# Softmax sums divided out once per pair of heads, on GpSimd by way of DRAM; four loads and one store moved to ScalarE's queue

## The chip, the cores and the metric

One core of a Trainium2 chip runs the program in one launch. The metric is device time in microseconds (us). The kernel before takes 1885.9 us (median of 3 runs, 1885.32 to 1886.08).

## The reference

One layer of a streaming encoder on x (1 x 1024 x 1024, fp32) and a conditioning vector c:

```
mod = silu(c) @ w_ada + b_ada                    # 9 vectors of 1024: shift, scale, gate, three times
h = rms(x) * (1 + scale) + shift;  x += 0.5 * gate * swiglu(h)        # FFN 1, D_FF = 2816
h = rms(x) * (1 + scale) + shift;  x += gate * mixer(h)
h = rms(x) * (1 + scale) + shift;  x += 0.5 * gate * swiglu(h)        # FFN 2
out = rms(x) * g_final

mixer:  p = h @ w_in                             # q, k, v of 8 attention heads x 64; q, k, v, o of 4 mLSTM heads x 128; gates
        first attention ("fox"):  logits = q k^T / 8 + cum(i) - cum(j), causal;  y_a = softmax(logits) v
        mLSTM ("ml"):  chunks of the matrix memory, causal conv before, norm and sigmoid gate after -> y_b
        return [y_a, y_b] @ w_out
```

## The kernel before

**Order.** Five engine programs run the parts one after another: FFN 1 (with the modulation of the start), mixer, output projection, FFN 2. Each fp32 product is three fp32r products, high x high, high x low and low x high; ScalarE cuts the high parts (`w_cut_hi`, `cut_hi`), VectorE or GpSimd the low ones (`w_cut_lo`, `cut_lo`). All order is written out by hand in the engines' programs and held by semaphores. There is no planner. All DMAs are issued by SyncE (SP), in one queue.

**First attention.** `mixer` goes through 4 pairs of heads (`PAIRS`), each with 8 blocks of 128 queries (`NS`), the longest block (1024 keys) first. For a block q of a pair p:
- TensorE: `scores` (L2872) of both heads into PSUM. `turn_prob` (L2887) transposes the exponentials by 128x128 pieces. `values` (L2903) multiplies the transposed pieces with v and gives y, by feature, in bank 6 + q % 2, columns 0 to 127. `turn_rinv` (L2909) transposes the inverse sums into columns 128 to 255 of the same bank. Projections of the next pair's q and k (L2132 to L2134) are put between.
- VectorE: `logits` (L2595) adds the decay rows `cum_bc` and takes the minimum; `invert` (L2614) makes the inverse of the row sums, spread over 128 columns; `keep_pt` (L2607) moves part of the transposed pieces; `normalise` (L2621) multiplies y by the turned inverses and writes `yT_fox`.
- ScalarE: `exp_rows` (L2385) with the row sums, `keep_pt` (L2393), `keep_rinv` (L2399), `keep_qk` (L2376 for k, L2374 for q).
- GpSimd: `mask_block` (L2287), one per block, on the causal block of `cum_bc`; it waits for the logits of the block before. At blocks 1 and 2 also one `w_cut_lo` (L2124). After the last pair: two `w_cut_lo` of the mLSTM's v weights, three of head weights, then the other mask `mask_m` (L2318, L2320), which VectorE awaits at L2690.
- SP: `fox_loads` per pair: wait for all logits of the pair before, load `cum_bc`, load the next pair's q and k weights; in pair 0 then spill x to `x_spill`. After the four pairs, four loads of v weights, then `head_load`, which waits for the low cuts of the pieces before it.

A block's y frees its bank by `y_done`. `values` of block q waits for `y_done` of block q - 2, and after the pair `project_q0` for all eight.

**Start.** `Start.load` issues the small rows, then x tiles 0 to 3 (L640) alternating with four pieces of w_ada (L636), then four more pieces, FFN 1's first weights (L432), and the second half of pieces. ScalarE squares and scales the x tiles (`act_lead`). VectorE sums the pieces (`dve_sum`, L808 to L816). FFN 1's first product (L1042 to L1044) needs both.

**End.** Output tiles 4 to 7 go out as halves: the right one scaled by ScalarE (`scale_half`, L1510), the left one by VectorE (L1733). SP issues all eight (L1378).

Of the kernel before, what the change touches and what calls it, by code (L numbers as in the profile page):

```python
# [14 lines left out]
P = 128  # L15
# [551 lines left out]
class Start:  # L567
# [55 lines left out]
    def load(self, sp, first_weights):  # L623
        KD, D = self.c.KD, self.c.D
        sp.dma_start(self.brow[2 * KD:, :], self.c_vec.rearrange("a (k p) -> (a k) p", p=P))\
            .then_inc(self.small_loaded, 16)
        sp.dma_start(self.brow[0:2 * KD, :], self.b_ada[:, 0:2 * D].rearrange("a (r n) -> (a r) n", n=P))\
            .then_inc(self.small_loaded, 16)
        columns = self.w_ada[0, :, 0:2 * D].rearrange("a (v h n) -> h a v n", v=2, h=2)

        def piece(half, k):
            if half:
                self.wait_piece(sp, 0, k)
                if k >= 4:
# [4 lines left out]
        def tile(t):  # L639
            sp.dma_start(self.c.xres[:, t, :], self.x[0, t * P:(t + 1) * P, :]).then_inc(self.x_loaded[t], 16)  # L640

        for k in range(4):
            tile(k)
            piece(0, k)
        for k in range(4, KD):
            piece(0, k)
        first_weights(0)
        for k in range(KD):
            piece(1, k)
        first_weights(1)  # L650
        for t in range(4, self.c.NS):
            tile(t)
# [87 lines left out]
    def act_lead(self, act):  # L740

        c, KD = self.c, self.c.KD
        act.wait_ge(self.b_turned, 1)
# [500 lines left out]
def ffn(core, tag, buf, halved, weights, w_out, spill, x_dram, gate_row, next_mod=None, g_final=None, out=None,  # L1244
# [53 lines left out]
    def sync(sp):  # L1298
# [71 lines left out]
        else:  # L1370
# [8 lines left out]
            sp.wait_ge(stored, 16 * (NS + 4))  # L1379
# [43 lines left out]
    def scalar(act):  # L1423
# [88 lines left out]
        if next_mod is None:  # L1512
# [13 lines left out]
            for t in (6, 7):  # L1526
                scale_half(t)
        else:
# [442 lines left out]
def mixer(core, ms, w_mix_in, b_fox_f, b_m_i, b_m_f, w_conv, b_conv, g_mhn, w_mix_out,  # L1971
# [57 lines left out]
    rinv_made, rinv_kept = s("rinv_made"), s("rinv_kept")  # L2029
# [48 lines left out]
    rinv = core.at("mx_rinv", [P, 4, P], 120)  # L2078
# [129 lines left out]
    def sync(sp):  # L2208
# [6 lines left out]

        def fox_loads(p, first, last):
# [11 lines left out]
        repeat(sp, PAIRS, fox_loads)  # L2228
        for piece in range(4):
            w_load(sp, piece % 2, C_MV[0] + piece // 2, w_in[:, 2 * piece:2 * piece + 2, COL_MV:COL_MV + MW])  # L2230

# [35 lines left out]
    def gpsimd(pool):  # L2267
# [49 lines left out]
        pool.wait_ge(y_done, PAIRS * NS)  # L2317
# [32 lines left out]
    def scalar(act):  # L2350
# [44 lines left out]
        def keep_rinv(p, q, first):  # L2395
            act.wait_ge(pv_ready, p * NS + (q + 1))
            if not (first and q < 2):
                act.wait_ge(y_done, p * NS + (q - 1))
            act.copy(rinv[:, 2 + q % 2, :], core.bank[:, 6 + q % 2, P:2 * P]).then_inc(rinv_kept, 1)  # L2399

        def fox_body(p, first, last):
            for q in range(1, NS + 1):
# [16 lines left out]
                if q > 1:  # L2419
                    keep_rinv(p, q - 2, first)  # L2420
                if q < NS:
                    keep_pt(p, 2 * q - 1, first)
            keep_rinv(p, NS - 1, first)
# [35 lines left out]
        def ml_body(h, first, last):  # L2459
# [27 lines left out]
            if h == 1:  # L2487
                act.wait_ge(x_spilled, NS * 16)
                for k in range(PAIRS):
# [39 lines left out]
    def vector(dve):  # L2529
# [79 lines left out]
        def invert(p, q, first):  # L2609

            dve.wait_ge(prob_done, p * PER + (2 * q + 2))
            if not (first and q < 2):
                dve.wait_ge(pv_ready, p * NS + (q - 1))
            dve.reciprocal(rinv[:, q % 2, :].rearrange("p (e d) -> p e d", e=2),  # L2614
                           rowsum[:, 2 * q:2 * q + 2].unsqueeze(2).to_broadcast([P, 2, HD]))\
                .then_inc(rinv_made, 1)

        def normalise(p, q):
            dve.wait_ge(rinv_kept, p * NS + (q + 1))
            i = BLOCK[2 * q]  # L2620
            dve.tensor_tensor(yT_fox[:, bass.ds(p, 1), i * P:(i + 1) * P].rearrange("p a s -> p (a s)"),  # L2621
                              core.bank[:, 6 + q % 2, 0:P], rinv[:, 2 + q % 2, :], ALU.mult).then_inc(y_done, 1)

        def fox_body(p, first, last):
            link.at(p)
            for q in range(1, NS + 1):
# [13 lines left out]
                if q > 1:  # L2640
                    normalise(p, q - 2)
            normalise(p, NS - 1)
# [149 lines left out]
    def tensor(pe):  # L2792
# [98 lines left out]
        def values(p, q, first):  # L2891
# [9 lines left out]
            for j in range(i + 1):  # L2901
                for e in range(2):
                    pe.matmul(bank[e * HD:(e + 1) * HD, 0:P], v_fox[:, j, bass.ds(p * (2 * HD) + e * HD, HD)],  # L2903
                              pt_of(2 * q + e, j * P, (j + 1) * P), start=(j == 0), stop=(j == i))
# [12 lines left out]
        def fox_body(p, first, last):  # L2917
            project_q0(p, first, range(2 if first else 0, KD - 2))
            for q in range(1, NS):
                scores(p, q, first)  # L2920
                if q in (6, 7):
                    values(p, q - 2, first)
                    turn_rinv(p, q - 2)
                    turn_prob(p, 2 * q - 2, first)
                else:
# [3 lines left out]
                    else:  # L2929
                        values(p, q - 2, first)  # L2930
                        turn_rinv(p, q - 2)
# [17 lines left out]
            turn_rinv(p, NS - 2)  # L2949
            turn_rinv(p, NS - 1)  # L2950
# [497 lines left out]
```

## Time and profile before

| | us |
|---|---|
| median of 3 runs | 1885.9 |
| the profiled execution's own time | 1886.72 |
| its span (first to last instruction) | 1885.0 |
| TensorE busy | 1856.6 (98%) |
| VectorE busy | 1183.5 (63%) |
| ScalarE busy | 764.7 (41%) |
| GpSimd busy | 841.3 (45%) |
| mean granted TensorE clock | 0.995 |

In the rows below, PE is TensorE, PEld its weight load, DVE VectorE, ACT ScalarE, POOL GpSimd, SPq the DMA issues of SyncE. Times are us from the start of the span, and L12 is line 12 of the kernel. Square brackets hold an engine's idle time before an instruction, and what ended it. "issue" there means that it waited for nothing that the profile shows. Matmuls are pipelined, so that the distance between two starts tells more than their durations. Busy shares of TensorE near 100% say that it has work queued, not that it runs at its peak.

The first attention lies at about 755 to 945 us; a pair takes about 50 us.

### The profile page before, as it was taken

The page shows a single profiled execution, that of the slowest core. Times are in us where ns is not written, and L with a number is a line of the kernel's source. Part 1 is how long each engine was busy: PE and PEld are TensorE (multiplying, and loading weights), DVE is VectorE, ACT ScalarE, POOL GpSimd, SP SyncE. Part 2 cuts the span into 40 slices and gives each one's busy share as a digit, 9 for nine tenths or more (in the row PEclk, how much of TensorE's full clock was granted, in tenths as well). Part 3 has the DMA queues.
Part 4 walks back from the last instruction along what each step waited for, and adds up shares of the span by engine and source line. Part 5 has one row for each costly group of instructions (what it writes and reads, how often), then busy time and mean ns, then how long its engine had stood idle before and what let it go on. Part 6 is the DMA issues. An engine that isn't in the chain of part 4 may idle for free.

```text
span 1885.0 us, 25322 instructions
## 1 busy us (share of the span) xinstructions
PE 1856.6 (98%) x9100; PEld 1527.7 (81%) x9100; DVE 1183.5 (63%) x1763; ACT 764.7 (41%) x1439; POOL 841.3 (45%) x635
## 2 busy tenths in 40 slices
PE   7999999999999999999999999999999999999998
PEld 6888888888888878777788888878888888888886
DVE  6966777666777782555604567477634454368678
ACT  5643232332444552555513555352333323334445
POOL 1588877783000111222222332699877887700003
PEclk8999999999999999999999999999999999999999
DMA  9346666654976401301112123424322422178652
GB/s 341 101 139 206 188 205 201 181 179 144 389 237 190 124 24 42 136 27 46 68 49 70 45 68 127 175 95 128 107 95 90 130 100 101 46 292 312 209 192 90
DMA packets 213379, 267.95 MB, mean 142 GB/s; under 512 B 16100, under 2 KB 126856, under 8 KB 212744
## 3 DMA queue, kind: packets, MB, share of 16 engines
q1 hardware_dynamic: 213256, 266.34, 42.4%
q8 instruction: 73, 1.20, 0.2%
q14 instruction: 50, 0.41, 0.1%
HBM read 211.17 MB, written 53.03 MB: 140 GB/s over the span
## 4 chain that ended last, share of the span: by engine, by line
PE 87%; DVE 5%; POOL 4%; issue 2%; ACT 1%; SPq 1%; DMA 1%; DVEq 0%; ACTq 0%; POOLq 0%
PE bank L1768 13%; PE bank L1769 13%; PE bank L1770 13%; PE bank L1202 6%; PE bank L1200 6%; PE bank L1201 6%; PE bank L2132 5%; PE bank L2134 5%; PE bank L2133 5%; PE bank L2903 2%; PE bank L2887 2%; PE bank L2872 1%; PE bank L1042 1%; PE bank L1043 1%; PE bank L1044 1%
## 5 line engine op out<-in xcount | busy, mean ns | idle before, releaser
L510 POOL TENSOR_TENSOR ffn_ring_b<-ffn_raw_in,ffn_ring_b 128x512 fp32r<-128x512 f32 x146 | 204.8, 1411 | 98.9 <-ACT ffn_ring_b L505 98.8
L1200 PE MATMUL bank<-ffn_w_hi,ffn_a_hi 128*128 128x512 f32 x616 | 239.7, 389 | 0.0
L1201 PE MATMUL bank<-ffn_w_lo,ffn_a_hi 128*128 128x512 f32 x616 | 239.6, 389 | 0.0
L1202 PE MATMUL bank<-ffn_w_hi,ffn_a_lo 128*128 128x512 f32 x616 | 239.6, 389 | 0.0
L132 POOL TENSOR_SCALAR rms<-rms 128x1 f32<-128x1 f32 x20 | 9.0, 449 | 427.5 <-ACT ffn_junk L124 419.6
L1155 ACT CAST ffn_a_hi<-ffn_a_stage 128x512 fp32r<-128x512 f32 x154 | 95.6, 621 | 200.7 <-PE bank L1202 195.4
L505 ACT CAST ffn_ring_b<-ffn_raw_in 128x512 fp32r<-128x512 f32 x150 | 92.4, 621 | 199.1 <-PE bank L1770 192.6
L510 POOL TENSOR_TENSOR ffn_ring_a_lo<-ffn_raw_in,ffn_ring_a_hi 128x512 fp32r<-128x512 f32 x106 | 146.5, 1393 | 54.9 <-ACT ffn_ring_a_hi L505 52.8
L1166 DVE TENSOR_TENSOR ffn_a_lo<-ffn_a_stage,ffn_a_hi 128x512 fp32r<-128x512 f32 x154 | 106.3, 690 | 72.1 <-ACT ffn_a_hi L1155 71.9
L2124 POOL TENSOR_TENSOR mx_w_lo<-mx_raw_w,mx_w_hi 128x1024 fp32r<-128x1024 f32 x25 | 59.8, 2390 | 176.8 <-ACT mx_w_hi L1886 113.3
L1547 DVE TENSOR_TENSOR ffn_u<-bank,ffn_u 128x512 f32<-128x512 f32 x103 | 70.8, 688 | 107.5 <-PE bank L1770 106.8
L1200 PEld LDWEIGHTS bank<-ffn_w_hi,ffn_a_hi 128*128 128x128 f32 x616 | 115.7, 188 | 24.4 <-DVE ffn_w_lo L1166 0.4
L1202 PEld LDWEIGHTS bank<-ffn_w_hi,ffn_a_lo 128*128 128x128 f32 x616 | 115.7, 188 | 24.0
L1201 PEld LDWEIGHTS bank<-ffn_w_lo,ffn_a_hi 128*128 128x128 f32 x616 | 115.7, 188 | 23.9
L1768 PE MATMUL bank<-h_hi,ffn_ring_a_hi 128*128 128x512 f32 x340 | 133.0, 391 | 1.1 <-DVE ffn_g L1547 0.5
L1770 PE MATMUL bank<-h_hi,ffn_ring_a_lo 128*128 128x512 f32 x340 | 132.3, 389 | 0.0
L1769 PE MATMUL bank<-h_lo,ffn_ring_a_hi 128*128 128x512 f32 x340 | 132.3, 389 | 0.0
L1769 PE MATMUL bank<-f_t_lo,ffn_ring_b 128*128 128x512 f32 x340 | 132.3, 389 | 0.0
L1768 PE MATMUL bank<-h_hi,ffn_ring_b 128*128 128x512 f32 x332 | 130.0, 392 | 0.4 <-ACT ffn_g L1431 0.2
L1770 PE MATMUL bank<-h_hi,ffn_ring_b 128*128 128x512 f32 x332 | 129.3, 389 | 0.0
L2132 PE MATMUL bank<-h_hi,mx_w_hi 128*128 128x512 f32 x296 | 118.5, 400 | 0.0
L1768 PE MATMUL bank<-f_t_hi,ffn_ring_b 128*128 128x512 f32 x300 | 116.8, 389 | 0.6 <-DVE f_t_lo L340 0.6
(427 smaller groups left out, 4690.1 us busy)
## 6 DMA issues: line engine op xcount, KB each, us to landing
ffn_raw_in<-in_w_ffn_in SPq DMA_DIRECT2D x84, 512.0 KB, 5.9
ffn_a_stage<-hidden SPq DMA_DIRECT2D x154, 256.0 KB, 3.6
ffn_w_stage<-in_w_ffn_out SPq DMA_DIRECT2D x132, 256.0 KB, 3.5
ada_rest<-in_w_ada SPq DMA_DIRECT2D x64, 448.0 KB, 3.8
hidden<-ffn_u SPq DMA_DIRECT2D x87, 256.0 KB, 2.0
hidden<-ffn_g SPq DMA_DIRECT2D x66, 256.0 KB, 2.0
mx_raw_w<-in_w_mix_in SPq DMA_DIRECT2D x28, 512.0 KB, 4.6
xres<-in_x SPq DMA_DIRECT2D x16, 512.0 KB, 8.1
```

What stands on the lines that cost most here:

```text
L510: pool.tensor_tensor(self.lo(q), self.source(b, m), self.hi(q).bitcast(F32), ALU.subtract)\
L1155: act.copy(self.op(self.buf.a_hi, n), self.a_source(n)).then_inc(self.hi_done, 1)
L1166: dve.tensor_tensor(self.op(lo, n), source, self.op(hi, n).bitcast(F32), ALU.subtract)\
L1200: pe.matmul(dst, a_hi, w_hi, start=first, stop=False, skip_group_check=True)
L1201: pe.matmul(dst, a_hi, w_lo, start=False, stop=False, skip_group_check=True)
L1202: return pe.matmul(dst, a_lo, w_hi, start=False, stop=True, skip_group_check=True)
L1768: pe.matmul(dst, w_hi, h_hi, start=(fresh and k == 0), stop=False, skip_group_check=True)
L1769: pe.matmul(dst, w_hi, h_lo, start=False, stop=False, skip_group_check=True)
L1770: mm = pe.matmul(dst, w_lo, h_hi, start=False, stop=(k == 3), skip_group_check=True)
L2132: pe.matmul(dst, a_hi, b_hi, start=start, stop=False, skip_group_check=skip)
L2133: pe.matmul(dst, a_hi, b_lo, start=False, stop=False, skip_group_check=skip)
L2134: return pe.matmul(dst, a_lo, b_hi, start=False, stop=stop, skip_group_check=skip)
```

## The change

Three things:
1. **Attention.** `invert` writes two numbers per token and block instead of 128. `turn_rinv`, `keep_rinv` and `normalise` go; VectorE copies the undivided y out of PSUM (`keep_y_fox`), and the last matmul of `values` carries `pv_ready`. After each pair SP stores the pair's 2048 inverses to DRAM, by token (one element of 4 bytes each), waits for the store, and loads them back as rows spread over 64 partitions per head (`spread_inverse`). GpSimd multiplies the pair's yT_fox by them, in place, in one instruction of 128x1024 (`divide`): behind block 4's mask of the next pair, and for the last pair behind the three head cuts, ahead of `mask_m`. SP's loop over the pairs is written out.
2. **Start.** x tiles 0 to 3 are issued by ScalarE, ahead of its first activation; SP issues the pieces of w_ada back to back.
3. **End.** The right halves of output tiles 6 and 7 go out as one DMA issued by ScalarE.

```diff
@@ Start.load / act_lead
-        for k in range(4):
-            tile(k)
-            piece(0, k)
-        for k in range(4, KD):
+        for k in range(KD):
             piece(0, k)
@@
+        for t in range(4):
+            self.load_tile(act, t)
         act.wait_ge(self.b_turned, 1)
@@ end of FFN 2: SP, then ScalarE
                 for half, done, n in ((1, half_scaled, t - 3), (0, norm.scaled, t + 1)):
+                    if half and t > 5:
+                        continue
@@
+            act.wait_ge(half_scaled, 4)
+            act.dma_start(out[0, 6 * P:8 * P, BANK:D].rearrange("(t p) d -> p t d", p=P), core.xres[:, 6:8, BANK:D])\
+                .then_inc(stored, 16)
@@ mixer
-    rinv = core.at("mx_rinv", [P, 4, P], 120)
+    rinv = core.at("mx_rinv", [P, PAIRS, 2 * NS], 120)
+    rinv_bc = core.at("mx_rinv_bc", [P, S], 16)
+    rinv_rows = nc.dram_tensor("rinv_rows", (PAIRS * 2 * S,), F32, kind="Internal").ap()
@@ SP
+        def spread_inverse(pairs):
+            before = pairs - 1
+            sp.wait_ge(rinv_made, pairs * NS)
+                sp.dma_start(rinv_rows[bass.ds(before * (2 * S), 2 * S)].rearrange("(n t) -> t n", t=P),
+                             rinv[:, bass.ds(before, 1), :].rearrange("p a n -> p (a n)")).then_inc(rinv_stored, 16)
+            sp.wait_ge(rinv_stored, pairs * 16)
+            sp.wait_ge(x_spilled, NS * 16)
+            if pairs > 1:
+                sp.wait_ge(y_divided, pairs - 1)
+            for e in range(2):
+                sp.dma_start(rinv_bc[e * HD:(e + 1) * HD, :],
+                             rinv_rows[bass.ds(before * (2 * S) + e * S, S)].partition_broadcast(HD)).then_inc(rinv_loaded, 16)
@@ fox_loads, behind the next pair's weights; and once behind the four loads of v weights
+            if not first:
+                spread_inverse(p)
@@ GpSimd
+        def divide(pairs):
+            part = yT_fox[:, bass.ds(pairs + -1, 1), :].rearrange("p a s -> p (a s)")
+            pool.wait_ge(y_done, pairs * NS)
+            pool.wait_ge(rinv_loaded, pairs * 32)
+            pool.tensor_tensor(part, part, rinv_bc[:, :], ALU.mult).then_inc(y_divided, 1)
@@ fox_cut
                 mask_block(p, q)
+                if q == 4 and not first:
+                    divide(p)
@@ after the head cuts
-        pool.wait_ge(y_done, PAIRS * NS)
+        divide(PAIRS)
         pool.memset(mask_m[:, :], 0.0).then_inc(late_mask_set, 1)
@@ ScalarE: keep_rinv and its calls are gone; it awaits y_divided before it reads yT_fox in head 1
@@ VectorE
-            if not (first and q < 2):
-                dve.wait_ge(pv_ready, p * NS + (q - 1))
-            dve.reciprocal(rinv[:, q % 2, :].rearrange("p (e d) -> p e d", e=2),
-                           rowsum[:, 2 * q:2 * q + 2].unsqueeze(2).to_broadcast([P, 2, HD]))\
-                .then_inc(rinv_made, 1)
+            inverse = rinv[:, bass.ds(p, 1), :].rearrange("p a (e i) -> p (a e) i", e=2)[:, :, i:i + 1]
+            dve.reciprocal(inverse, rowsum[:, 2 * q:2 * q + 2].unsqueeze(2)).then_inc(rinv_made, 1)
-        def normalise(p, q):
-            dve.wait_ge(rinv_kept, p * NS + (q + 1))
-            dve.tensor_tensor(yT_fox[...], core.bank[:, 6 + q % 2, 0:P], rinv[:, 2 + q % 2, :], ALU.mult).then_inc(y_done, 1)
+        def keep_y_fox(p, q):
+            dve.wait_ge(pv_ready, p * NS + (q + 1))
+            dve.tensor_copy(yT_fox[...], core.bank[:, 6 + q % 2, 0:P]).then_inc(y_done, 1)
@@ TensorE
+            mm.then_inc(pv_ready, 1)
-        def turn_rinv(p, q):
-            bank = core.bank[:, 6 + q % 2, :]
-            pe.wait_ge(rinv_made, p * NS + (q + 1))
-            pe.transpose(bank[:, P:2 * P], rinv[:, q % 2, :], core.ident[:, :]).then_inc(pv_ready, 1)
```

## Rows read from the trace of the kernel before

**Rows 1.** The page's chain that ended last, shares of the span by engine.

```profile
PE 87%; DVE 5%; POOL 4%; issue 2%; ACT 1%; SPq 1%; DMA 1%; DVEq 0%; ACTq 0%; POOLq 0%
```

**Rows 2.** Busy time by stretch: length, engines (x instructions), clock, DMA share, GB/s.

```profile
28.00:30.00 2.00, 2.00 (x6) 1.56 (x5) 2.00 (x4) 1.94 (x4) 0.00 (x0) 0.50 1.05 407
...
800.00:850.00 50.00, 49.66 (x391) 39.30 (x390) 26.76 (x76) 25.76 (x62) 10.58 (x10) 1.00 0.12 39
...
1883.00:1884.00 1.00, 0.00 (x0) 0.00 (x0) 0.00 (x0) 0.00 (x0) 0.00 (x0) 0.50 1.03 399
```

**Rows 3.** TensorE's waits, 755 to 1160: us in total, times, longest.

```profile
PE bank L3007 <- POOL mx_w_lo L2124: 0.9, 3, 0.3
PE bank L2872 <- DVE mx_fk_lo L2572: 0.7, 3, 0.2
```

**Rows 4.** Timeline, block 2 of pair 0: start, duration, engine, line.

```profile
766.69 1.97 PE L2903 MATMUL bank<-mx_probT,mx_v_fox 128*64 128x128 f32 x32
...
768.59 0.33 PE L2909 MATMUL bank<-ident,mx_rinv 128*128 128x128 f32 x1
...
768.75 0.93 PE L2887 MATMUL bank<-ident,mx_prob 128*128 128x128 f32 x7
...
769.61 0.50 PE L2872 MATMUL bank<-mx_fk_hi,mx_fq_hi 64*128 64x512 f32 x2
```

**Rows 5.** Timeline, end of pair 1.

```profile
854.46 0.50 PE L2872 MATMUL bank<-mx_fk_hi,mx_fq_hi 64*128 64x512 f32 x2 [0.23 <-DVE mx_fk_lo L2572]
```

**Rows 6.** Timeline, end of the last pair.

```profile
943.77 0.44 PE L2909 MATMUL bank<-ident,mx_rinv 128*128 128x128 f32 x2
...
943.97 0.48 PE L2132 MATMUL bank<-mx_w_hi,h_hi 128*128 128x512 f32 x1
```

**Rows 7.** Groups of instructions by line, 755 to 945.

```profile
L2614 DVE RECIPROCAL mx_rinv<-mx_rowsum 128x128 f32<-128x128 f32 x32 | 30.4, 949 | 0.7 <-ACT mx_prob L2385 0.7
```

**Rows 8.** Timeline, GpSimd and VectorE in pairs 0 and 1.

```profile
765.96 0.95 DVE L2595 CUSTOM_DVE_ANT_0 mx_prob<-bank,mx_cum_bc 128x768 f32<-128x768 f32 x1
...
767.32 0.95 DVE L2595 CUSTOM_DVE_ANT_0 mx_prob<-bank,mx_cum_bc 128x768 f32<-128x768 f32 x1
...
767.75 2.37 POOL L2124 TENSOR_TENSOR mx_w_lo<-mx_raw_w,mx_w_hi 128x1024 fp32r<-128x1024 f32 x1 [2.90 <-ACT mx_w_hi L1886]
...
827.33 0.73 POOL L2287 TENSOR_TENSOR mx_cum_bc<-mx_cum_bc,mx_mask_m 128x256 f32<-128x256 f32 x1 [3.15 <-DVE mx_low L2595]
```

**Rows 9.** Timeline, SP in pair 2, GpSimd and ScalarE after the pairs.

```profile
848.39 1.00 SPq L1875 DMA_DIRECT2D mx_raw_w<-in_w_mix_in  x2
...
953.64 2.39 POOL L2124 TENSOR_TENSOR mx_w_lo<-mx_raw_w,mx_w_hi 128x1024 fp32r<-128x1024 f32 x1 [17.31 <-ACT mx_w_hi L1886]
...
971.55 1.05 ACT L1886 CAST mx_w_hi<-mx_raw_w 128x1024 fp32r<-128x1024 f32 x1 [9.83 <-PE bank L2134]
```

**Rows 10.** DMA issues: operands, queue, count, KB each, us to landing.

```profile
gate_rows<-mx_rows_out SPq DMA_DIRECT2D x1, 48.0 KB, 1.5
...
ffn_shift_columns<-mod_rows SPq DMA_DIRECT2D x1, 4.0 KB, 6.7
```

**Rows 11.** Timeline, first mLSTM head.

```profile
997.98 0.17 DVE L2690 TENSOR_TENSOR mx_tiny<-mx_m_max,mx_mst 128x8 f32<-128x8 f32 x1 [5.93 <-POOL mx_mask_m L2320]
...
1001.47 2.60 DVE L2707 SCALAR_TENSOR_TENSOR mx_mkT<-mx_pre_k,mx_consts,mx_mkT 128x1024 f32<-128x1024 f32 x2
...
1006.10 4.62 DVE L2707 SCALAR_TENSOR_TENSOR mx_mqT<-mx_pre_q,mx_consts,mx_mqT 128x1024 f32<-128x1024 f32 x2
...
1020.24 1.15 ACT L2481 ACTIVATE mx_mkT<-mx_mkT,mx_consts 128x1024 f32<-128x1024 f32 x1
```

**Rows 12.** Timeline, the start.

```profile
0.80 1.28 ACT L744 ACT_TABLE_LOAD   x1 [0.80 <-PEq L3437]
...
1.65 0.41 SPq L640 DMA_DIRECT2D xres<-in_x  x1
...
15.40 1.28 DVE L816 SCALAR_TENSOR_TENSOR ada_lead_acc<-ada_ring,c_act,ada_lead_acc 128x1024 f32<-128x1024 f32 x1 [0.61 <-DMA ada_ring<-in_w_ada]
```

More of the change, by code:

```diff
@@ L651, in load, with load_tile @@
         for t in range(4, self.c.NS):
-            tile(t)
+            self.load_tile(sp, t)
+    def load_tile(self, eng, t):
+        eng.dma_start(self.c.xres[:, t, :], self.x[0, t * P:(t + 1) * P, :]).then_inc(self.x_loaded[t], 16)
     def sums_by(self, pieces):
@@ L1378, in sync @@
                     sp.dma_start(out[0, t * P:(t + 1) * P, cols], core.xres[:, t, cols]).then_inc(stored, 16)
-            sp.wait_ge(stored, 16 * (NS + 4))
+            sp.wait_ge(stored, 16 * (NS + 3))
     def gpsimd(pool):
@@ L2214, in sync @@
         sp.wait_ge(rows_stored, 16)
+        def spread_inverse(pairs):
+            before = pairs - 1
+            sp.wait_ge(rinv_made, pairs * NS)
+            with nc.allow_non_contiguous_dma(reason="inverse sums by token, 16 columns"):
+                sp.dma_start(rinv_rows[bass.ds(before * (2 * S), 2 * S)].rearrange("(n t) -> t n", t=P),
[7 more added lines that the diff above has]
+                             rinv_rows[bass.ds(before * (2 * S) + e * S, S)].partition_broadcast(HD)).then_inc(rinv_loaded, 16)
         def fox_loads(p, first, last):
@@ L2226, in fox_loads @@
                     sp.dma_start(x_spill[t * P:(t + 1) * P, :], core.xres[:, t, :]).then_inc(x_spilled, 16)
-        repeat(sp, PAIRS, fox_loads)
+        for p in range(PAIRS):
+            fox_loads(p, p == 0, p == PAIRS - 1)
         for piece in range(4):
             w_load(sp, piece % 2, C_MV[0] + piece // 2, w_in[:, 2 * piece:2 * piece + 2, COL_MV:COL_MV + MW])
+        spread_inverse(PAIRS)
         def head_load(m):
@@ L2393, in keep_pt @@
             act.copy(pt_of(n, 0, w), turned_bank(n, 0)[:, 0:w]).then_inc(pt_act, 1)
-        def keep_rinv(p, q, first):
-            act.wait_ge(pv_ready, p * NS + (q + 1))
-            if not (first and q < 2):
-                act.wait_ge(y_done, p * NS + (q - 1))
-            act.copy(rinv[:, 2 + q % 2, :], core.bank[:, 6 + q % 2, P:2 * P]).then_inc(rinv_kept, 1)
         def fox_body(p, first, last):
@@ L2611, in invert @@
             dve.wait_ge(prob_done, p * PER + (2 * q + 2))
-            if not (first and q < 2):
-                dve.wait_ge(pv_ready, p * NS + (q - 1))
-            dve.reciprocal(rinv[:, q % 2, :].rearrange("p (e d) -> p e d", e=2),
-                           rowsum[:, 2 * q:2 * q + 2].unsqueeze(2).to_broadcast([P, 2, HD]))\
-                .then_inc(rinv_made, 1)
-        def normalise(p, q):
-            dve.wait_ge(rinv_kept, p * NS + (q + 1))
-            i = BLOCK[2 * q]
-            dve.tensor_tensor(yT_fox[:, bass.ds(p, 1), i * P:(i + 1) * P].rearrange("p a s -> p (a s)"),
-                              core.bank[:, 6 + q % 2, 0:P], rinv[:, 2 + q % 2, :], ALU.mult).then_inc(y_done, 1)
+            i = BLOCK[2 * q]
+            inverse = rinv[:, bass.ds(p, 1), :].rearrange("p a (e i) -> p (a e) i", e=2)[:, :, i:i + 1]
+            dve.reciprocal(inverse, rowsum[:, 2 * q:2 * q + 2].unsqueeze(2)).then_inc(rinv_made, 1)
+        def keep_y_fox(p, q):
+            dve.wait_ge(pv_ready, p * NS + (q + 1))
+            i = BLOCK[2 * q]
+            dve.tensor_copy(yT_fox[:, bass.ds(p, 1), i * P:(i + 1) * P].rearrange("p a s -> p (a s)"),
+                            core.bank[:, 6 + q % 2, 0:P]).then_inc(y_done, 1)
         def fox_body(p, first, last):
@@ L2640, in fox_body @@
                 if q > 1:
-                    normalise(p, q - 2)
-            normalise(p, NS - 1)
+                    keep_y_fox(p, q - 2)
+            keep_y_fox(p, NS - 1)
             if not last:
@@ L2902, in values @@
                 for e in range(2):
-                    pe.matmul(bank[e * HD:(e + 1) * HD, 0:P], v_fox[:, j, bass.ds(p * (2 * HD) + e * HD, HD)],
-                              pt_of(2 * q + e, j * P, (j + 1) * P), start=(j == 0), stop=(j == i))
-        def turn_rinv(p, q):
-            bank = core.bank[:, 6 + q % 2, :]
-            pe.wait_ge(rinv_made, p * NS + (q + 1))
-            pe.transpose(bank[:, P:2 * P], rinv[:, q % 2, :], core.ident[:, :]).then_inc(pv_ready, 1)
+                    mm = pe.matmul(bank[e * HD:(e + 1) * HD, 0:P], v_fox[:, j, bass.ds(p * (2 * HD) + e * HD, HD)],
+                                   pt_of(2 * q + e, j * P, (j + 1) * P), start=(j == 0), stop=(j == i))
+            mm.then_inc(pv_ready, 1)
         def first_mv(t, ks):
```

13 lines of the change are left out of this document (3 added, 10 removed).

## The prediction

> **What bounds the kernel now.** I read the chain of waits first: 87% of the span is TensorE's own work [rows 1]. So a change saves time only where it shortens TensorE's queue, or where TensorE waits. Then the table by stretch, for the attention: in 50 us TensorE is busy 49.66 at clock 1.00, while VectorE has 26.8 and ScalarE 25.8 [rows 2]. Then TensorE's waits from 755 to 1160: the two longest groups come to 0.9 and 0.7 us [rows 3]. The attention is bound by TensorE's instruction stream, not by the engines that the change relieves. Last I read the timeline around each instruction that goes or is moved, and the first and last 30 us, where DMA is the bound: 407 GB/s at 28 to 30 us, 399 in the last full microsecond of the end [rows 2].
>
> **The change part by part.**
>
> *TensorE, the 32 transposes of inverse sums.* What one costs is its slot, not its 0.33 us. In a block the 32 matmuls of values begin 0.055 apart ((1.97 - 0.27 of the last) / 31), so the last begins at 768.39; the transpose begins at 768.59 and the next real one at 768.75 [rows 4]. So the last matmul of values and turn_prob are 0.36 apart. Without turn_rinv a wait still stands between them, that of turn_prob. What such a boundary costs is seen one step on: the seven transposes (0.11 apart) have their last start at about 769.41, and scores begin at 769.61, 0.20 later; values to turn_rinv is 0.20 too [rows 4]. So the boundary stays at 0.20 and each transpose gives back 0.16. Blocks 2 to 7 of each of the 4 pairs have one such place (turn_rinv of the block two before): 24 x 0.16 = 3.8 us. The other two transposes of a pair come at its end. In pairs 0 to 2 TensorE waits there for VectorE's low cut of k (scores at 854.46, idle 0.23 for fk_lo) [rows 5], which follows from the projection and not from the transposes: 3 x 0. In the last pair nothing is awaited: 943.77 to 943.97, 0.20 us [rows 6]. Sum 4.0 us. Bounds: nothing, if the next wait (ScalarE's copy of the piece before) ends no earlier; or the whole 0.36 at 24 places and 0.4 at the last, 9 us, if the boundary closes too. I take 4.0, since both boundaries in the row agree, and in block 2 the copy that turn_prob awaits had ended 0.4 us ahead of it.
>
> *VectorE and ScalarE.* invert shrinks from 949 ns [rows 7] to about 0.17 (an operation of 8 columns takes 0.17 [rows 11]), 32 x 0.78 = 25 us of VectorE; 32 copies of ScalarE go (0.26 each in the timeline); normalise becomes a copy of the same size. All of it lies beside TensorE's stream, so I put it at 0. It widens margins: y_done comes earlier, and nobody waited for it. A gain of up to 0.7 us is possible where TensorE awaited fk_lo [rows 3]; a loss I exclude, for both engines only get less.
>
> *SP, spread_inverse.* In pairs 1 to 3 it stands behind the next weights, which are issued by 849.4 in pair 2 [rows 9]; SP's next task is a pair (50 us) away, so its waits hold up nobody there. What matters is when the rows land. No row shows a store of 2048 single elements. From both sides: 48 KB of rows stored took 1.5 us; 1024 single elements loaded took 6.7, behind 1 MB of other loads [rows 10]. So 1.5 to 13.4 (twice 6.7); I take 4, nearer to the store. With the load back (5 us at most for 512 KB; the larger loads of this shape took 4.9 in the DMA table) the rows are there 9 us after 849.4, 18 us at the latest, 868. divide comes at 874.5 in that pair. Hidden. After the last pair SP waits at about 941 for the last inverses, and head_load(0) behind it waited until 956 in any case, for the cut that began at 953.64 [rows 9]. So 15 us of store cost nothing; even then the weight is first cut at 971.55, 10 us after it lands [rows 9]. Cost 0.
>
> The Trainium skill says in "DMA: Bandwidth & Descriptors" (Rules for kernel authors; Specifications) that a strided last dimension becomes one descriptor per element and that transfers under 512 B are read, changed and written back. It speaks against this store, and no row here shows such a store. By it the store would lie at the slow end; the sum stays until some 20 us, and this rule is why the slow store below has a chance at all.
>
> *GpSimd, divide.* A tensor_tensor of 128x1024 takes 2.37 [rows 8]. In pair 1 it stands between mask 4 (ends about 824.2) and mask 5, which begins at 827.33 after 3.15 us of idling [rows 8]: it fits with 0.7 us to spare, in pairs 1 to 3 alike. Without that cover it would put up to 2.4 us in front of VectorE's logits, three times. The last one goes ahead of mask_m: VectorE, idle 5.93 us for the mask, goes on at 1000.4 instead of 997.98; its convolution of k ends near 1007.7, and ScalarE takes it up at 1020.24 [rows 11]. 12 us of cover. Cost 0.
>
> GpSimd may also slow VectorE: a pair of convolution steps takes 2.60 alone and 4.62 beside a GpSimd cut [rows 11]. But logits of the same width take 0.95 without and 0.95 beside a GpSimd operation of 2.37 [rows 8]. divide runs beside logits. Cost 0, upper end 2.0 a pair.
>
> By the skill's "GPSIMD Engine Reference" (Key points) the two engines contend where VectorE has two SBUF inputs. Logits have one, the other being PSUM, and the convolution has two; the trace agrees with both (0.95 and 0.95; 2.60 and 4.62). By this rule the three divides are free, and the last one might lengthen a convolution that has 12 us.
>
> *Start.* ScalarE could begin its work at 0.80 [rows 12], SP issued the first tile at 1.65 [rows 12], and from about 3 us on DMA is the bound. The stream can begin up to 0.85 earlier; the order of bytes (tile and piece by turns) stays. VectorE's sums awaited a piece at 15.40 [rows 12] and ran densely from there to FFN 1's first product at 27.3, so an earlier piece counts. But TensorE runs at 0.50 until about 32 [rows 2], and if that moment doesn't move, only about half of the lead is kept (a matmul of 512 columns comes every 0.43 there and every 0.23 after it). The four issues push the table load back by 2 us, c_act from 3.3 to some 4.1; its first use was at 6.9, when the piece had landed. I take 0.5; bounds -0.85 of gain and 0.5 of loss (if tiles and pieces get in each other's way).
>
> *End.* All data were ready at 1880.6, and the last issue at 1881.7; that looks like 1 us to gain. But the 16 engines ran at 383 to 414 GB/s from 1880 until 1884 (399 in the last of the four [rows 2]). The same bytes remain, so 0 (bounds -0.3 and +0.3).
>
> **Sum.** 4.0 + 0 + 0.5 + 0 = 4.5 us off the profiled execution's span of 1885.0 and its own time of 1886.72, so 1882.2 for it. It lay 0.8 above the median; 1885.9 - 4.5 = 1881.4.
>
> **The rivals.**
> 1. *The boundary closes too* (the 0.20 also goes, or VectorE's relief shortens waits called "issue"): 9 + 0.5, 1876.4. For it: the gap isn't named by any releaser. Against: it is 0.20 behind values and behind transposes alike [rows 4].
> 2. *The next wait takes its place*: turn_prob needs ScalarE's copy; TensorE's stream then is no shorter, and only the start remains: 1885.4. Against: the 0.4 us margin in block 2, and more in the later blocks.
> 3. *GpSimd's divide stalls VectorE* (other side): in block 4 to 5 of pairs 1 to 3, logits stretched as the convolution is, 3 x 2.0, and mask 5 pushed by what exceeds 0.7 us of room, 3 x 1.0 more when GpSimd itself gets slower by that much. 1885.9 - 4.5 + 6.0 = 1887.4, to 1890.4. It decides from 1.5 us a pair (4.5 / 3). Against: 0.95 and 0.95 [rows 8].
> 4. *The store is slow*: free up to 20 us in the pairs and about 24 after the last; from there every us counts fully, 30 us would give 1881.4 + 6 + 3 x 10 = 1917. Each of 16 engines has 128 elements, so it would need 0.16 us an element; 6.7 us for 1024 of them [rows 10] says less than 0.11 even with all of the queue ahead charged to them.
> 5. *The start's half clock moves*: the 12 matmuls at half clock cost 12 x 0.20 = 2.4 us; with them gone 1879.0, with as many more 1883.8. The clock there fell while TensorE had few matmuls, and the new order of arrivals changes these.
>
> **Chances.** Forecast 0.60 (own range 1880 to 1883), rival 1 0.10, rival 2 0.12, rival 3 0.06, rival 4 0.02, rival 5 0.10. A range from 1877.5 to 1884.5 takes in the forecast, rival 5 and part of 1 and 2. What a measurement can tell from no change is 0.2%, 3.8 us: faster means below 1882.1. The forecast is near that line: three quarters of its 0.60, rival 1 and half of rival 5 give 0.60 faster; slower takes rival 4 and most of rival 3, 0.07; the same is the rest, 0.33.
>
> **What would show it.** L2909 gone, and the last matmul of values and turn_prob 0.20 apart (0.36: rival 2; 0.06: rival 1). A pair at 49.3 instead of 50.3 us. Mask 5 without a later start relative to the logits before it, and logits of 512 columns at 0.69 beside divide (longer: rival 3). The store's landing between 1.5 and 13.4 us. The first FFN matmul at 26.5 to 27.3. The last byte out at the same distance from the last matmul as before. The prediction is wrong if TensorE's waits in the attention pass 2 us, or if the pair's length doesn't change.

## The result, and the profile after

The changed kernel takes 1890.3 us (median of 9 runs, 1889.69 to 1892.37); the kernel before took 1885.81 beside it (9 runs, 1884.9 to 1886.85). The ratio is 1.0025, 95% interval 1.0016 to 1.0033: slower by 4.5 us, where 1881.4 and a gain of 4.5 were forecast. The measurement also lies outside the range of 1877.5 to 1884.5.

Its profiled execution took 1889.85, with a span of 1887.6. I set the two traces side by side at three places: the first scores of the attention, the first scores of the last pair, and TensorE's first matmul behind the last values and transposes (943.97 before [rows 6], 946.36 after).

| stretch of the span, us | before | after | difference |
|---|---|---|---|
| to the first scores | 755.04 | 753.03 | -2.01 |
| pairs 0 to 2 (scores to scores) | 149.77 | 147.84 | -1.93 |
| last pair, to the first matmul behind it | 39.16 | 45.49 | +6.33 |
| from there to the end | 941.03 | 941.24 | +0.21 |

The first two parts gained, the start more than its forecast of 0.5, the three pairs less than theirs (18 x 0.16 = 2.9). The part behind the pairs hardly moved. The last pair lost three times what either of the first two gained. The place is seen in TensorE's waits from 740 to 1030 (us in total, times, longest), which answer to [rows 3]:

```profile
PE bank L2912 <- issue: 5.5, 1, 5.5
PE bank L2897 <- DVE mx_fk_lo L2599: 1.8, 3, 0.6
```

One new wait of 5.5 us, put down to "issue": TensorE waited for a semaphore whose release the profile does not name. The timeline of that moment shows what it was. In the kernel before, SP issued the v weights early in this pair, and ScalarE cut them without waiting:

```profile
898.39 66.19 SPq L1875 DMA_DIRECT2D mx_raw_w<-in_w_mix_in  x6
...
910.24 1.03 ACT L1886 CAST mx_w_hi<-mx_raw_w 128x1024 fp32r<-128x1024 f32 x1
```

SP's queue in the last pair of the changed kernel (start, duration, line, operands):

```profile
895.37 0.37 SPq L2228 DMA_DIRECT2D rinv_rows<-mx_rinv  x1
907.23 1.09 SPq L2235 DMA_DIRECT2D mx_rinv_bc<-rinv_rows  x2
908.37 15.74 SPq L1879 DMA_DIRECT2D mx_raw_w<-in_w_mix_in  x4
```

and TensorE and ScalarE around that wait, then TensorE behind the pair:

```profile
908.21 1.09 PE L2912 MATMUL bank<-ident,mx_prob 128*128 128x128 f32 x8
...
906.20 0.18 ACT L2420 ACTIVATION_READ_ACCUMULATOR mx_prob<-mx_prob,mx_low 128x1 f32 x1
914.58 1.04 ACT L1890 CAST mx_w_hi<-mx_raw_w 128x1024 fp32r<-128x1024 f32 x1 [8.20 <-DMA mx_raw_w<-in_w_mix_in]
915.53 0.58 ACT L2428 COPY mx_probT<-bank 128x512 f32<-128x512 f32 x1
...
916.21 1.94 PE L2912 MATMUL bank<-ident,mx_prob 128*128 128x128 f32 x8 [5.51 <-issue]
...
946.36 0.50 PE L2139 MATMUL bank<-mx_w_hi,h_hi 128*128 128x512 f32 x1
```

Read from the top: SP stores the inverse sums of pair 2 and waits for them, 895.37 to 907.23. Behind it in SP's program stand, in this pair, the four loads of the v weights, which the kernel before issued from 898.39 on and this one at 908.37. ScalarE's program has the cut of these weights between an exponential and the copy keep_pt. It comes to the cut at 906.4 and waits 8.20 us for the DMA. TensorE's next transposes need the bank that keep_pt empties: the copy begins at 915.53, and they begin at 916.21. TensorE has stopped for 5.51 us of ScalarE's 8.20, so it had 2.7 us of cover. Behind the stall the granted clock is down (columns: the stretch, its length, TensorE busy and its instructions, clock, DMA share, GB/s):

```profile
905.00:910.00 5.00, 5.00 (x33) 1.00 0.27 81
910.00:915.00 5.00, 0.70 (x4) 0.79 0.74 234
915.00:920.00 5.00, 3.79 (x20) 0.52 0.01 2
920.00:925.00 5.00, 5.00 (x62) 1.00 0.16 25
```

At 915 to 920 it is 0.52, next to the lower of the two levels, 1.2 of 2.4 GHz: the transposes at 916.21 take 1.94 us for eight, 1.09 for eight at full clock at 908.21.

The DMA table of the page (operands, queue, count, KB each, us to landing) shows what held SP, and the count of packets shows why:

```profile
DMA packets 222257, 270.06 MB, mean 143 GB/s; under 512 B 24468, under 2 KB 135224, under 8 KB 221624
rinv_rows<-mx_rinv SPq DMA_DIRECT2D x4, 8.0 KB, 13.3
mx_rinv_bc<-rinv_rows SPq DMA_DIRECT2D x8, 256.0 KB, 3.9
```

Before, 16100 packets were under 512 B. The 8368 more are the 4 x 2048 elements of the stores and 176 others. By "DMA: Bandwidth & Descriptors" (Rules for kernel authors) of the Trainium skill a strided last dimension becomes one descriptor per element; the traces agree. Run 2 below, which differs from the changed kernel only in storing rows of 16 adjacent elements (512 rows instead of 8192 elements), has 7679 packets under 512 B fewer than the changed kernel, and run 7, which stores 2048 single elements once, has 2065 more than the kernel before.

### The profile page after: what moved, and what is told of

Same layout as the page of the kernel before. It is cut to its first block, busy times and chain, and to the rows that moved or that the text cites. A ratio compares the mean times of both kernels' runs of the same rounds, so it can differ in the third digit from the quotient of the medians.

```text
span 1887.6 us, 25171 instructions
## 1 busy us (share of the span) xinstructions
PE 1853.4 (98%) x9068; PEld 1525.1 (81%) x9068; DVE 1157.8 (61%) x1763; ACT 758.0 (40%) x1407; POOL 849.4 (45%) x639
## 4 chain that ended last, share of the span: by engine, by line
PE 87%; DVE 4%; POOL 4%; issue 2%; DMA 1%; ACT 1%; SPq 0%; DVEq 0%; ACTq 0%; POOLq 0%
PE bank L1772 13%; PE bank L1773 13%; PE bank L1774 13%; PE bank L1199 6%; PE bank L1200 6%; PE bank L1201 6%; PE bank L2139 5%; PE bank L2141 5%; PE bank L2140 5%; PE bank L2912 2%; PE bank L2897 2%; PE bank L2928 2%; POOL out_xn L157 1%; PE bank L3317 1%; PE bank L3315 1%
```

## The experiments

Each was timed against the kernel before on the same chip (its medians there: 1884.92 for the first four, 1884.78 for the next four, 1885.1 for the last). My theory after the traces: the wait on the store, ahead of the v weights, is the whole loss. The rivals: something in the change itself (the divide, GpSimd's order) slows the last pair; or the clock does, for a reason of its own.

**1. The call moved behind the first two v weights.**

```
-            if not first:
+            if not first and not last:
                 spread_inverse(p)
...
         for piece in range(4):
             w_load(...)
+            if piece == 1:
+                spread_inverse(PAIRS - 1)
```

> The changed kernel, with one call moved: the third spread_inverse stands behind the issues of the first two pieces of the v weights instead of ahead of all four. Theory (the store of the inverse sums, 10.5 to 15.4 us to its landing, holds SP and with it the v weights, ScalarE's cut of them waits 8.20 us in its in-order stream and TensorE's pieces of turned probabilities with it): TensorE's stall at 911 to 920 and the half clock behind it go, the last pair falls from 44.75 to about 37.5 us and the time by 7.2, from 1890.3 to 1883.1 (1882 to 1884.5). Rival A (the last pair is slow because of the divide or of GpSimd's order, not of SP's): the pair stays over 42 us, time over 1888. Rival B (the clock falls there for another reason): the stall goes but some 2 us of half clock stay, 1885.

Measured: 1881.26 (1880.52 to 1881.67), 3.66 below the kernel before, ratio 0.998 [0.9971, 0.9989]. Against the changed kernel, each taken from its own kernel before, that is 4.5 + 3.66 = 8.1 us. The expected 1883.1 was missed by 1.8, and the time lies below the expected range: about 0.9 of it is that the kernel before ran 0.9 faster here (1884.92 against 1885.81), and 0.9 that the stall costs 8.1 by the medians, where the expectation reckoned with 7.2. SP's queue, then ScalarE and TensorE in the same pair:

```profile
892.91 0.95 SPq L1879 DMA_DIRECT2D mx_raw_w<-in_w_mix_in  x2
893.90 0.56 SPq L2228 DMA_DIRECT2D rinv_rows<-mx_rinv  x1
907.84 1.10 SPq L2235 DMA_DIRECT2D mx_rinv_bc<-rinv_rows  x2
915.77 0.89 SPq L1879 DMA_DIRECT2D mx_raw_w<-in_w_mix_in  x2
```

```profile
899.38 0.50 PE L2899 MATMUL bank<-mx_fk_hi,mx_fq_hi 64*128 64x512 f32 x2 [0.59 <-DVE mx_fk_lo L2601]
...
904.80 1.03 ACT L1890 CAST mx_w_hi<-mx_raw_w 128x1024 fp32r<-128x1024 f32 x1
...
909.02 1.03 PE L2914 MATMUL bank<-ident,mx_prob 128*128 128x128 f32 x8
...
937.67 0.50 PE L2139 MATMUL bank<-mx_w_hi,h_hi 128*128 128x512 f32 x1
```

The store is as slow as before (13.94 us from issue to the loads behind it), but nobody waits: ScalarE cuts at 904.80 without idling, the granted clock is 1.00 in every window of 5 us from 905 to 935, and the pair is 937.67 - 899.38 = 38.29 us long, 7.2 less than in the changed kernel. Rivals A and B both fall. The stall isn't of one length: in run 3 below, which has the changed kernel's order, ScalarE waited 10.20 and TensorE 7.5 us. There it was 7.7 us from the issue of the v weights to ScalarE's cut, and 6.2 in the changed kernel's profile.

**2. The store as rows.**

```
-                sp.dma_start(rinv_rows[...].rearrange("(n t) -> t n", t=P), ...)
+                sp.dma_start(rinv_rows[...].rearrange("(t n) -> t n", t=P), ...)
```

> The changed kernel in its own order, with the store of the inverse sums written as 64 bytes a partition (16 adjacent elements) instead of 2048 single elements; the results of the first attention are then divided by sums of other tokens. Theory (the single elements make the store long): it lands in 1.5 to 3 us, the v weights are issued about 9 us earlier in the last pair, ScalarE's wait falls from 8.2 to under 1 us, and the time is 1883.1 to 1884. Rival (the store's time is a fixed latency of writing to DRAM and of the semaphore, or the queue ahead of it): it lands at over 8 us as before and the time stays at 1889 to 1890.5.

Measured: 1881.02 (1880.5 to 1882.27), 3.90 below the kernel before (ratio 0.998 [0.9971, 0.9989]), with SP in the changed kernel's order. This kernel leaves out the turn from tokens to rows, so that its quotients are of other tokens' sums; its work is otherwise the same. It has 16789 packets under 512 B. Its SP queue:

```profile
844.63 3.10 SPq L2228 DMA_DIRECT2D rinv_rows<-mx_rinv  x1
852.32 1.09 SPq L2235 DMA_DIRECT2D mx_rinv_bc<-rinv_rows  x2
894.24 0.33 SPq L2228 DMA_DIRECT2D rinv_rows<-mx_rinv  x1
897.80 1.40 SPq L2235 DMA_DIRECT2D mx_rinv_bc<-rinv_rows  x2
899.24 17.81 SPq L1879 DMA_DIRECT2D mx_raw_w<-in_w_mix_in  x4
934.44 0.34 SPq L2228 DMA_DIRECT2D rinv_rows<-mx_rinv  x1
935.86 1.09 SPq L2235 DMA_DIRECT2D mx_rinv_bc<-rinv_rows  x2
```

The last store has nothing ahead of it and is awaited for 1.4 us; that in the last pair, behind the load of cum_bc, 3.6; those behind two weights of 512 KB, 6.6 and 7.7. In the changed kernel the same four are 10.5, 11.9, 15.4 and 14.8. The differences are 9.1, 8.3, 8.8 and 7.1 us: that is what single elements cost, and the rest is the queue ahead. So the theory stood in its conclusion and was too low in its 1.5 to 3 us, which left out the queue; its 1883.1 to 1884 was missed like run 1's, for the same two reasons. The v weights go out at 899.24 and the stall is gone.

**3 and 4. The attention alone, as it was changed, and with the call moved.** Start and end as in the kernel before; the fourth has the edit of the first.

> The change in the attention alone; start and end as in the kernel before. Theory (the start brought 2.0 us, the end nothing): 1890.3 + 2.0 = 1892.3. Rival (what the start gains is given back later, so it counts 0.5 as forecast): 1890.8.

> The change in the attention alone, with the third spread_inverse behind the first two pieces of the v weights. Theory: four pairs at 0.64 each and nothing else, 1885.8 - 2.6 = 1883.2; if start's 2.0 added to it fully, then the kernel with both would be 1881.2, so the difference between this and the fixed kernel with the new start shows what the start is worth behind the attention. Rival (a transpose is worth the 0.16 forecast as soon as nothing else stands in the way): 1885.8 - 4.0 = 1881.8. Rival (the attention's gain is lost again behind it): 1885.

Measured: 1891.5 (1889.55 to 1891.9; 6 runs, ratio 1.0032 [1.002, 1.0044]), and 1882.39 (1881.53 to 1883.27; ratio 0.9987 [0.9978, 0.9996]). Run 3 lies 6.6 above its kernel before, 2.1 more than the changed kernel does. That is the 2.0 of its theory, but by luck: the premise that the start brings 2.0 isn't borne out by runs 4 and 5, and run 3's profile shows a stall 2 us longer. The attention without its stall gives 2.53 us (the fourth's theory had 2.6), and the stall costs 9.1 in this pair of kernels. In the fourth's trace the attention is 2.73 shorter than before. The first rival of the fourth (0.16 a transpose) asked for 1881.8, 4.0 under a before of 1885.8; against the 1884.92 measured beside it that is 1880.9, below all of its runs. It falls, and so does the third (1885).

**5. The start alone**, the kernel before otherwise: ScalarE issues the first four tiles of x, SP only pieces.

```
-        for k in range(4):
-            tile(k)
-            piece(0, k)
-        for k in range(4, KD):
+        for k in range(KD):
             piece(0, k)
...
+        for t in range(4):
+            self.load_tile(act, t)
         act.wait_ge(self.b_turned, 1)
```

> The kernel before with the change of the start alone: the first four tiles of x issued by ScalarE's queue, all the pieces by SP's. Theory (the pieces land earlier and the first FFN matmul with them; the fixed kernel with this start was 1.1 below the one without): 1884.9 - 1.1 = 1883.8. Rival (the 2.0 us between the two traces at the first scores is all the start's): 1882.9. Rival (my forecast of 0.5): 1884.4. Rival (the start's gain in the traces is only a shorter stretch of half clock, which differs from execution to execution): 1884.9.

Measured: 1883.73 (1883.1 to 1884.68), 1.05 below the kernel before; the interval of the ratio, 0.9985 to 1.0003, just takes in no change. The difference between runs 1 and 4, which differ in the start and the end, gives 1.13, so I take it as about 1.1. None of the four values that were on record is excluded by these intervals; the medians speak for the theory's 1.1. What the profiles show besides is TensorE's first matmul of FFN 1, here before and in this run:

```profile
27.34 0.77 PE L1042 MATMUL bank<-h_hi,ffn_ring_a_hi 128*128 128x512 f32 x1 [1.20 <-DVE mod_cols L835]
```

```profile
26.13 0.77 PE L1041 MATMUL bank<-h_hi,ffn_ring_a_hi 128*128 128x512 f32 x1 [0.77 <-DVE mod_cols L834]
```

It comes at 27.04 to 27.41 in the six profiles with the old start, and at 25.65 to 26.26 in the five with the new one: 1.2 us apart by their medians, without overlap. What follows hides this in a single pair of traces. The mean granted clock from 18 to 34 us is 0.57 in the kernel before, 0.79 in run 4 with the same start, and 0.68, 0.68 and 1.00 in the changed kernel, this run and run 1, all three with the new start. The first scores do not simply follow it: they come at 751.46 here (0.68), 751.56 in run 1 (1.00) and 753.03 in the changed kernel (0.68). In FFN 1 TensorE also waits for `ffn_g` once, 0.5 us in the profile of the kernel before and 0.8 in that of the changed one, and not in those of runs 1 and 5. So the 2.01 of the table is a difference of two executions with such waits in each, and one profiled execution can't price this edit.

**6. The end alone**: ScalarE issues the last two right halves as one DMA (the diff of the change).

> The kernel before with the change of the end alone: ScalarE issues the last two right halves as one DMA. Theory (the last 4 us move 397 to 410 GB/s whoever issues them): no change, 1884.9, within 0.3. Rival (one issue less on SP and less waiting for it): 1883.9.

Measured: 1885.05 (1884.16 to 1885.41), 0.27 above the kernel before, ratio 1.0000 [0.9991, 1.0009]. No change can be told, as forecast; the rival's 1883.9 lies below all runs.

**7. The wait alone, in the kernel before.**

```
+            if last:
+                sp.dma_start(scratch_rows.rearrange("(n t) -> t n", t=P), core.ident[:, 0:2 * NS])\
+                    .then_inc(scratch_stored, 16)
+                sp.wait_ge(scratch_stored, 16)
```

> The kernel before with nothing of the change but one thing added in the last pair: SP stores 128x16 elements singly to DRAM and waits for the store ahead of the v weights. Theory (that wait alone makes the changed kernel slow): the v weights are issued some 12 us later, near 910.8, land near 917.0, and ScalarE, at its cut from 910.24 on, waits 6.8 us (8.20 in the changed kernel, which reaches the cut earlier); TensorE stalls 5.5 - 1.4 = 4.1 us and runs at half clock after it for 1.7 more: 1884.9 + 5.8 = 1890.7. Rival (the changed kernel's pair was slow through something in the change itself): under 1886.5.

Measured: 1890.51 (1890.2 to 1891.74; 7 runs), 5.7 above the kernel before, ratio 1.0031 [1.002, 1.0042]; 5.8 was expected. Its SP queue, its ScalarE, and TensorE's longest wait:

```profile
896.98 0.43 SPq L2225 DMA_DIRECT2D scratch_rows<-ident  x1
910.14 14.05 SPq L1875 DMA_DIRECT2D mx_raw_w<-in_w_mix_in  x4
```

```profile
915.03 1.04 ACT L1886 CAST mx_w_hi<-mx_raw_w 128x1024 fp32r<-128x1024 f32 x1 [6.12 <-DMA mx_raw_w<-in_w_mix_in]
```

```profile
PE bank L2894 <- issue: 3.4, 1, 3.4
```

None of the change is in this kernel, and it has the same kind of loss, 5.7 of the changed kernel's 8.1. In the trace the last pair is 947.56 - 903.40 = 44.16 us long instead of 39.16: 5.0 more, of which 3.4 are the stall (4.1 was expected) and 1.6 come behind it (1.7 was expected). The windows 915 to 920 and 920 to 925 show a clock of 0.71 and 0.95 there; ScalarE's work that was put off is done there too, and I haven't separated the two. The other 0.7 of the 5.7 isn't in this pair of profiles.

The three stalls on record fit one another. ScalarE's wait, TensorE's stall and the growth of the last pair are 6.12, 3.4 and 5.0 here; 8.20, 5.5 and 7.2 in the changed kernel against run 1; 10.20, 7.5 and 9.3 in run 3 against run 4 (47.63 and 38.30 us). TensorE has 2.7 us of cover each time, and 1.6 to 1.8 us come behind the stall. So the part of the loss that this run lacks is a shorter wait of ScalarE: the v weights were issued 6.7 us behind the pair's first scores instead of 7.5, and from their issue to the cut it was 4.9 us instead of 6.2. The changed kernel loads `mx_rinv_bc` (512 KB) directly ahead of the weights and this one doesn't, which may be the reason; no run isolates it.

**8. GpSimd's work for the division doubled**, on top of run 1.

```
+            pool.tensor_tensor(rinv_bc[:, :], rinv_bc[:, :], rinv_bc[:, :], ALU.mult).then_inc(squared, 1)
+            ...
             pool.tensor_tensor(part, part, rinv_bc[:, :], ALU.mult).then_inc(y_divided, 1)
```

> The changed kernel with the third spread_inverse behind the first two pieces of the v weights, and GpSimd's work for the division doubled: each divide is preceded by a tensor_tensor of 128x1024 that squares the inverses (so the results are divided twice). The divide has 0.7 us of room before the next mask, the doubling asks 2.4. Theory (the mask is 1.7 us late, and VectorE, which is busy about half of the time in a pair, makes it up before TensorE needs it): 1881.3, within 0.5. Rival (every microsecond of a late mask reaches TensorE, as my third rival had it): 3 x 1.7 = 5.1 more, 1886.4. Behind the last pair 12 us of cover hold either way.

Measured: 1881.04 (1880.45 to 1881.95), against 1881.26 for run 1. As the expectation says, its results are divided twice. GpSimd in pair 2:

```profile
869.96 1.89 POOL L2323 TENSOR_TENSOR mx_rinv_bc<-mx_rinv_bc 128x1024 f32<-128x1024 f32 x1
872.11 2.37 POOL L2326 TENSOR_TENSOR mx_yT_fox<-mx_yT_fox,mx_rinv_bc 128x1024 f32 x1 [0.26 <-POOL mx_rinv_bc L2323]
874.43 0.74 POOL L2315 TENSOR_TENSOR mx_cum_bc<-mx_cum_bc,mx_mask_m 128x256 f32<-128x256 f32 x1
```

The mask runs directly behind the second one, without idling, 5.16 us behind the mask before it (869.27); in run 1 these are 3.77 apart (868.92 and 872.69). So it is 1.4 us late, and TensorE's waits are those of run 1 (1.8 us in three for fk_lo). VectorE makes it up. So the third rival's price for a late mask was wrong. What stretched logits would have cost isn't tested, for they weren't stretched.

**9. Each transpose of inverse sums issued twice, in the kernel before.**

```
             pe.wait_ge(rinv_made, p * NS + (q + 1))
+            pe.transpose(bank[:, P:2 * P], rinv[:, q % 2, :], core.ident[:, :])
             pe.transpose(bank[:, P:2 * P], rinv[:, q % 2, :], core.ident[:, :]).then_inc(pv_ready, 1)
```

> The kernel before with each of the 32 transposes of inverse sums issued twice, one directly after the other. Theory (a removed transpose gave back 0.11 us, the distance at which transposes follow each other, since the wait at the boundary stays whole and moves to the next one): the added ones cost the same 0.11 at 24 places and 2 x 0.11 behind the last pair, and the six at the other pairs' ends are taken up by the 0.23 of waiting there: 2.9 more, 1887.7; a pair gets 0.66 longer. Rival (0.16 apiece, as forecast): 24 x 0.16 + 0.3 = 4.1 more, 1888.9, a pair 0.96 longer. Rival (TensorE's slack takes them up): under 1 more.

Measured: 1887.78 (1886.7 to 1888.48) against 1885.1, 2.7 more where 2.9 were expected; ratio 1.0014 [1.0005, 1.0023]. The rivals' 1888.9 and under 1886.1 lie outside its runs. Block 2 of pair 0, and the first scores of pairs 1 and 2:

```profile
766.72 0.33 PE L2909 MATMUL bank<-ident,mx_rinv 128*128 128x128 f32 x1
766.88 0.27 PE L2910 MATMUL bank<-ident,mx_rinv 128*128 128x128 f32 x1
766.99 0.93 PE L2887 MATMUL bank<-ident,mx_prob 128*128 128x128 f32 x7
...
802.85 0.50 PE L2872 MATMUL bank<-mx_fk_hi,mx_fq_hi 64*128 64x512 f32 x2
...
853.83 0.50 PE L2872 MATMUL bank<-mx_fk_hi,mx_fq_hi 64*128 64x512 f32 x2
```

The first transpose behind the boundary takes a slot of 0.16, the second one of 0.11. Pair 1 is 853.83 - 802.85 = 50.98 long instead of 50.36, 0.62 more, or 0.10 for each of the six.

## Why the prediction was wrong, step by step

**The step that failed: SP, spread_inverse.** It said that the call stands behind the next weights in pairs 1 to 3, that "SP's next task is a pair (50 us) away, so its waits hold up nobody there", and put the cost at 0. This holds in pairs 1 and 2. In pair 3 there are no next q and k weights; the loop's last body is left at once, and the four loads of the v weights follow. They went out at 898.39 before and ScalarE cut them in block 1 of the same pair, at 910.24: the slack was 12 us less the transfer's 6. The prediction rests on SP's row in pair 2 [rows 9] and on those behind the pairs. The row of pair 3, at 898.39 (`mx_raw_w` six times), was there to be read. Measured for the step: +8.1 us (run 1 against the changed kernel), +9.1 with the old start (runs 3 and 4), +5.7 for the wait by itself (run 7). It decided the sign. TensorE's waits in the attention came to 5.5 + 1.8 = 7.3 us, past the 2 us that the prediction named as a sign of being wrong.

**The store's time**, taken as 4 us with bounds of 1.5 and 13.4, was 10.5 to 15.4, past the upper bound where 1 MB of weights was ahead of it. My upper bound doubled a row of 1024 elements [rows 10], queue and all; the right form is a sum: 1.4 us, 7 to 9 more for the elements and up to 6.3 for the queue ahead. In the pairs the price that I gave (free to 20 us) still holds: the rows were wanted at 871.10 in pair 2 and the loads issued at 860.60. The rival "the store is slow" had the right cause with the wrong threshold: it asked when the rows are needed, and not who stands behind SP.

**The transposes**, taken as 24 x 0.16 + 0.20 = 4.0, gave 2.5 (medians) to 2.8 (traces). The answer to [rows 4] in the changed kernel:

```profile
764.66 1.97 PE L2928 MATMUL bank<-mx_probT,mx_v_fox 128*64 128x128 f32 x32
766.56 0.98 PE L2912 MATMUL bank<-ident,mx_prob 128*128 128x128 f32 x7
767.48 0.50 PE L2897 MATMUL bank<-mx_fk_hi,mx_fq_hi 64*128 64x512 f32 x2
```

Values to scores: 2.92 us before (766.69 to 769.61), 2.82 now, so 0.10 to 0.11 given back. The boundary stayed at 0.20, as I had said: (1.97 - 0.27) / 31 = 0.055 puts the last matmul of values at 766.36. What I missed is that the first transpose behind a boundary has the longer slot: take the first one away, and the next one is the first (0.92 for the seven instead of 0.86). The slot to subtract is that of one among its like, 0.11, and run 9 adds it the same way. By the prediction's own signs rivals 1 and 2 fall (the distance is 0.20, not 0.06 or 0.36), and still its 0.16 was wrong: a pair became 0.63 to 0.67 us shorter and not 1.0. Six a pair make 0.66; the profiles show 0.67 in pair 0 (49.06 to 48.39) and 0.63 in pairs 1 and 2. In the last pair it is 6 x 0.11 + 0.20 = 0.86, and run 1 shows 39.16 - 38.29 = 0.87.

**The pairs' ends** at 3 x 0 were right, and for the reason given: TensorE waits for the low cut of k, 0.59 now where it was 0.23 [rows 5]. Of the removed transposes' time there only the wait is left:

```profile
801.42 0.50 PE L2897 MATMUL bank<-mx_fk_hi,mx_fq_hi 64*128 64x512 f32 x2 [0.59 <-DVE mx_fk_lo L2599]
```

**VectorE and ScalarE** at 0: the reciprocals fell from 949 [rows 7] to 163 ns, VectorE's busy time from 800 to 850 from 26.76 to 20.89 us [rows 2], and nothing came of it, as said. The changed kernel's rows:

```profile
L2641 DVE RECIPROCAL mx_rinv<-mx_rowsum 128x2 f32<-128x2 f32 (+1 forms) x32 | 5.2, 163 | 3.2 <-ACT mx_prob L2420 3.2
```

```profile
800.00:850.00 50.00, 49.29 (x391) 39.05 (x392) 20.89 (x76) 24.36 (x55) 12.91 (x11) 1.00 0.21 55
```

**The divide** at 0 was right, with the 0.7 us of room that the prediction named:

```profile
871.10 2.38 POOL L2321 TENSOR_TENSOR mx_yT_fox<-mx_yT_fox,mx_rinv_bc 128x1024 f32 x1
874.18 0.73 POOL L2313 TENSOR_TENSOR mx_cum_bc<-mx_cum_bc,mx_mask_m 128x256 f32<-128x256 f32 x1 [0.71 <-DVE mx_low L2622]
...
929.50 0.69 DVE L2622 CUSTOM_DVE_ANT_0 mx_prob<-bank,mx_cum_bc 128x512 f32<-128x512 f32 x1
```

The logits beside a divide take 0.69, as those of the same width took before (875.97, 876.90), so they aren't stretched (the divide of that pair ran from 927.99 to 930.37). This row is better evidence than the prediction's own: of the logits at 767.32 only the last 0.5 us lay beside the GpSimd operation that began at 767.75 [rows 8]. Run 8 shows that even the room wasn't needed. **The last divide** at 0: the stretch behind the pairs is 0.21 longer in all. **The start** was taken as 0.5 and is about 1.1 by the medians (run 5), though 0.5 isn't excluded. The lead at FFN 1's first matmul is 1.2 where at most 0.85 was reckoned with, and about all of it arrives instead of half; why the lead is larger stays open. Rival 5 (the half clock moves) can't be told apart from it: the matmuls at the half clock's distance (0.40 us or more from one start to the next) number 6 to 13 in the six profiles with the old start and 6 to 11 in the five with the new one. **The end** at 0 was right (run 6).

The terms now: 2.5 (run 4) + 1.1 (run 5) + 0 (run 6) = 3.6 of gain, and run 1, which has all of the change but the stall, measures 3.66. The failed step's 8.1 is itself the difference between run 1 and the changed kernel, so that the sum then gives the measured 4.5 slower says nothing more. The checks on it from outside are run 7's 5.7, run 3's and 4's 9.1, and the 7.2 of the profiles. Had the step held, the forecast gain would have been 0.8 us too large. Run 1 is the version that beats both kernels: 1881.26, 0.2% below the kernel before and 8.1 us below the changed one, each taken from its own kernel before.

## What to carry to other kernels

When a wait is put into an in-order queue, list what stands behind it in every iteration, the first and the last by themselves: in the last one, the next task may be another phase's load, with its consumer close. Issue first what somebody soon waits for, and the slow store behind it. What a removed instruction gives back is the slot of one among its like, not that of the one behind the wait, and a gain at a place where the engine waits anyway only lengthens that wait.

## What the runs showed of the hardware

- A store of 128x16 single elements from SBUF costs 7.1 to 9.1 us over the same bytes as 64 B rows, which with an empty queue are awaited for 1.4 us. As an estimate from these: if the 2048 elements spread evenly over the 16 DMA engines, they are 128 each, and one costs 0.055 to 0.071 us.
- Behind two weight loads (1 MB), the small store waits another 5.2 to 6.3 us for the queue (6.6 and 7.7 against 1.4).
- A stall of 5.5 us of TensorE brought the granted clock down to its lower level by the window 915 to 920 (0.52); the eight transposes behind it took 1.94 instead of 1.09. A stall of 3.4 us (run 7) was followed by windows at 0.71 and 0.95, one of 7.5 us (run 3) by 0.55 and 0.77.
- The half clock of the first 35 us differs between executions: 0.57 and 0.79 from 18 to 34 us in two profiles with the old start (before, run 4), 0.68 and 1.00 in two with the new one (runs 5 and 1). The first scores differ by 1.5 us between the first two and by 0.1 between the others. A difference of 1 or 2 us at the start can't be read from one trace of each kernel.
- A wait at a boundary between two groups of small matmuls costs 0.20 us between starts, and the first transpose behind it 0.05 more than its followers.
